# Gathering tokens for 32 experts from two fp32r parts instead of three bf16 parts

## The reference

```
g_idx = argmax(xt @ w_rg + b_rg)                      # 1 group of 4
top_val, top_idx = top_k(e_sel, 2)                    # 2 experts of the group's 8
gates = softmax(g_logits)[g_idx] * softmax(top_val)
# per expert e, over its own tokens xb:
hid = silu(xb @ w_gate[e]) * (xb @ w_up[e])           # 1024 -> 512
y = (hid @ w_down[e]) * gate                          # 512 -> 1024
out = segment_sum(y, token)                           # added back to the tokens' rows
```

## Time and profile before

| | |
|---|---|
| median of 3 runs | 2879.21 us (2877.5 to 2879.88) |
| profiled execution | 2876.93 us, of which 2875.7 us are the span from first to last instruction |
| granted TensorE clock, mean | 0.959 of 2.4 GHz |
| TensorE matmuls busy | 2737.2 us (95%) |
| TensorE weight loads busy | 1894.1 us (66%) |
| VectorE, ScalarE, GpSimd busy | 1221.8, 910.1, 367.7 us |
| moved by DMA | 543.60 MB |

### The profile page before, as it was taken

How to read it: one execution, slowest core, us unless ns; L and a number is a source line. 1 busy time by engine, 2 the same in 40 slices (tenths; PEclk the granted TensorE clock), 3 DMA queues, 4 the chain that set the end, 5 groups by cost and what they waited for, 6 DMA issues and landing times. The chain is left out here.

```text
span 2875.7 us, 36485 instructions
## 1 busy us (share of the span) xinstructions
PE 2737.2 (95%) x14944; PEld 1894.1 (66%) x14944; DVE 1221.8 (42%) x2275; ACT 910.1 (32%) x1666; POOL 367.7 (13%) x197
## 2 busy tenths in 40 slices
PE   7989999999878999999979999999999999999998
PEld 5865455444757545544467767788887776788887
DVE  1542223223755222322246652552553674356254
ACT  4331101111473111111154543442344454343233
POOL 3200000000330000000030011222222001122122
PEclk9989999999988999999999978999999996899999
DMA  5147999998315799999722011223232101123312
GB/s 203 61 188 314 406 402 407 397 406 340 103 44 200 310 406 406 400 402 406 320 85 74 30 59 44 88 88 106 71 109 68 65 17 57 54 79 102 104 59 81
DMA packets 134825, 543.60 MB, mean 189 GB/s; under 512 B 14592, under 2 KB 26112, under 8 KB 85376
## 3 DMA queue, kind: packets, MB, share of 16 engines
q1 hardware_dynamic: 127120, 536.94, 48.4%
q10 hardware_dynamic: 7536, 4.28, 0.5%
HBM read 539.09 MB, written 2.10 MB: 188 GB/s over the span
## 5 line engine op out<-in xcount | busy, mean ns | idle before, releaser
L500 PE MATMUL ps<-w,w 128*128 128x512 f32 x3360 | 769.7, 391 | 19.2 <-POOL w L256 10.1
L500 PEld LDWEIGHTS ps<-w,w 128*128 128x128 f32 x3360 | 632.5, 188 | 153.7 <-DVE w L443 9.8
L256 POOL TENSOR_TENSOR w<-w,w 128x1024 fp32r<-128x1024 f32 (+3 forms) x139 | 339.0, 2450 | 2267.1 <-ACT w L248 2267.1
L502 PE MATMUL ps<-w,w 128*128 128x512 f32 (+2 forms) x2256 | 495.5, 381 | 24.5 <-DVE w L981 15.2
L502 PEld LDWEIGHTS ps<-w,w 128*128 128x128 f32 x2256 | 415.4, 190 | 102.5 <-ACT w L572 15.6
L1185 PE MATMUL ps<-w,w 128*64 128x512 f32 x2048 | 451.6, 594 | 1.8 <-issue 1.8
L248 ACT ACTIVATE w<-w 128x1024 fp32r<-128x1024 f32 (+3 forms) x260 | 251.4, 1000 | 428.0 <-PE ps L500 221.5
L256 DVE TENSOR_TENSOR w<-w,w 128x1024 fp32r<-128x1024 f32 (+3 forms) x121 | 195.2, 1619 | 403.3 <-ACT w L248 400.8
L1185 PEld LDWEIGHTS ps<-w,w 128*64 128x64 f32 x2048 | 146.0, 137 | 285.5 <-issue 285.5
L1410 DVE TENSOR_TENSOR X<-ps,X 128x512 f32<-128x512 f32 x256 | 163.9, 682 | 221.5 <-PE ps L1221 220.5
L1207 PE MATMUL ps<-w,w 128*64 128x512 f32 x1024 | 226.8, 595 | 0.8 <-ACT w L1262 0.8
(11 more groups left out here) (234 smaller groups left out, 2305.4 us busy)
## 6 DMA issues: line engine op xcount, KB each, us to landing
w<-in_moe_w_gate SPq DMA_DIRECT2D x128, 1024.0 KB, 10.2
w<-in_moe_w_up SPq DMA_DIRECT2D x128, 1024.0 KB, 12.9
w<-in_moe_w_down SPq DMA_DIRECT2D x128, 1024.0 KB, 8.1
w<-in_w_up SPq DMA_DIRECT2D x40, 1024.0 KB, 5.1
w<-in_w_down SPq DMA_DIRECT2D x20, 1024.0 KB, 5.1
w<-in_w_in SPq DMA_DIRECT2D x16, 1024.0 KB, 5.1
w<-in_ab_w_in SPq DMA_DIRECT2D x10, 1024.0 KB, 5.1
w<-in_c_w_in SPq DMA_DIRECT2D x8, 1024.0 KB, 5.9
```

The lines of the kernel that those rows point to most:

```text
L256: up(self.wlo[self.low[s][0]], lane.e.tensor_tensor(lo, raw, hi.bitcast(F32), ALU.subtract))
L500: ins = pe.matmul(bank[:, :], wp[:, k, P * o:P * o + P], ap(k0 + k), start=first, stop=stop)
L502: ins = pe.matmul(bank[:, 0:width], ap(k0 + k)[:, P * o:P * o + P], wp[:, k, :], start=first, stop=stop)
```

## The change

The parts of the rows are two fp32r ones: ScalarE makes `HB[0]` (fp32r), VectorE the rest `HB[1]` (fp32r). The one-hot matrix stays bf16 as VectorE writes it; ScalarE copies each pair's `SEL` to an fp32r matrix `SELR` (`scalar_pick`), of which there is one buffer, and the gather reads that. `YH` and `YL` have one buffer instead of two. In the routing, `M8` and `MASK` are computed before the weights of the two choices. The small tiles move in SBUF into the region of the transposed features, and GpSimd's copy of the bf16 identity waits for the masks. The loop for overfull experts is changed in the same way.

```diff
-        HB = [at(2048 * j, 4, 1024, dt=BF16) for j in range(3)]
+        HB = [at(0, 4, 1024, dt=F32R), at(4096, 4, 1024, dt=F32R)]
...
+        SELR = at(S0 + 960, 4, P, dt=F32R)
...
-        YH = [at(10240, 1024, dt=F32R), at(11264, 1024, dt=F32R)]
-        YL = [at(12288, 1024, dt=F32R), at(13312, 1024, dt=F32R)]
+        YH = at(10240, 1024, dt=F32R)
+        YL = at(11264, 1024, dt=F32R)
...
         def tensor_gather(p, j):
-            PE.wait_ge(pick, p + 1)
+            PE.wait_ge(pick_r, p + 1)
...
-                for q in range(3):
+                for q in range(2):
                     for c in range(NT):
                         kk = 4 * j + k
-                        i = pe.matmul(bank[:, P * k:P * k + P], HB[q][:, c, P * kk:P * kk + P], SEL[p % 2][:, c, :],
-                                      start=(q == 0 and c == 0), stop=(q == 2 and c == NT - 1))
+                        i = pe.matmul(bank[:, P * k:P * k + P], HB[q][:, c, P * kk:P * kk + P], SELR[:, c, :],
+                                      start=(q == 0 and c == 0), stop=(q == 1 and c == NT - 1))
...
         def tensor_slots(p):
+            PE.wait_ge(cb_ready, 3)
             PE.wait_ge(gate3, 1)
+            PE.wait_ge(pick, p + 1)
...
+        def scalar_pick(p):
+            S.wait_ge(pick, p + 1)
+            if p:
+                S.wait_ge(bga.full, p)
+                S.wait_ge(bgv.full, p)
+            up(pick_r, act.activation(SELR[:, :, :], SEL[p % 2][:, :, :], ACT.Copy))
...
-            for j in range(2):
-                for c in range(NT):
-                    if j:
-                        S.wait_ge(hb_rest, c + 1)
-                    else:
-                        normed(S, c + 1)
-                    up(hb, act.activation(HB[j][:, c, :], HF[:, c, :], ACT.Copy))
+            for c in range(NT):
+                up(hb, act.activation(HB[0][:, c, :], HF[:, c, :], ACT.Copy))
...
+            scalar_pick(0)
             scalar_gather(0)
             for p in range(PAIRS):
+                if p + 1 < PAIRS:
+                    scalar_pick(p + 1)
                 bank = bg.next(S)
...
-            V.wait_ge(ba.free, 4)
-            for j in range(2):
-                for c in range(NT):
-                    V.wait_ge(hb, 4 * j + c + 1)
-                    dst = HF if j == 0 else HB[2]
-                    ins = dve.tensor_tensor(dst[:, c, :], HF[:, c, :], HB[j][:, c, :], ALU.subtract)
-                    up(h_row if j else hb_rest, ins)
+            for c in range(NT):
+                V.wait_ge(hb, c + 1)
+                up(h_row, dve.tensor_tensor(HB[1][:, c, :], HF[:, c, :], f32(HB[0][:, c, :]), ALU.subtract))
...
             up(rx_in, dve.tensor_tensor(ed, m2, m1, ALU.subtract))
+            vstep(dve.tensor_tensor(M8, O1, O2, ALU.add))
+            up(masks, dve.tensor_tensor(by_group(MASK), M8.unsqueeze(2).to_broadcast([P, 4, 4, 8]), groups, ALU.mult))
             V.wait_next(rx_out)
...
-            for a, name in ((tri_b, "tri"), (ones_b, "ones"), (identb, "ident")):
+            for a, name in ((tri_b, "tri"), (ones_b, "ones")):
                 up(cb_ready, pool.tensor_copy(a, cst(name)))
+            G.wait_ge(masks, 1)
+            up(cb_ready, pool.tensor_copy(identb, cst("ident")))
```

More of the change, by code:

```diff
@@ L1025, in program @@
         handoff(n) for n in ("gate", "up", "gather_act", "gather_dve", "hidden", "down", "slots"))
-    h_normed, cb_ready, hb, hb_rest, h_row = (
-        sig(n) for n in ("h_normed", "cb_ready", "h_bf16", "h_rest", "h_row"))
+    h_normed, cb_ready, hb, h_row = (sig(n) for n in ("h_normed", "cb_ready", "h_hi", "h_lo"))
     rx_in, rx_out, masks, n_ready = (
         sig(n) for n in ("router_exp_in", "router_exp_out", "masks", "n_ready"))
-    pick, st, yhi_w, gate3 = (sig(n) for n in ("pick", "slots_t", "y_hi_w", "gate3"))
+    pick, pick_r, st, yhi_w, gate3 = (sig(n) for n in ("pick", "pick_fp32r", "slots_t", "y_hi_w", "gate3"))
     def plan_moe(layer):
@@ L1075, in moe @@
         late = range(next_half + 3, next_half + SPLITS)
-        HB = [at(2048 * j, 4, 1024, dt=BF16) for j in range(3)]
+        HB = [at(0, 4, 1024, dt=F32R), at(4096, 4, 1024, dt=F32R)]
         HF = HF_[layer]
-        HTF = at((12288, 8192)[layer], KD, T)
+        S0 = (12288, 8192)[layer]
+        HTF = at(S0, KD, T)
         gB, WR = loaded.pop(("moe", layer))
-        CB = at(7168, 3, P, dt=BF16)
-        tri_b, ones_b, identb = CB[:, 0, :], CB[:, 1, :], CB[:, 2, :]
+        identb = at(S0 + 1728, P, dt=BF16)[:, :]
+        CB = at(16384, 2, P, dt=BF16)
+        tri_b, ones_b = CB[:, 0, :], CB[:, 1, :]
         R0 = 17408
@@ L1092, in moe @@
         MASK = at(R0 + 464, 4, 32, dt=BF16)[:, :, :]
[L1093 to L1102, removed]
+        CNT = at(16512, 32)[:, :]
+        CMP = at(16544, 32, NOVER)[:, :, :]
+        gr = at(16768, 2, 4, 32)
+        SID = at(S0, 4, 32)[:, :, :]
+        GATE = at(S0 + 128, 4, 32)[:, :, :]
+        OE = at(S0 + 256, 32)[:, :]
+        OS = at(S0 + 288, 32)[:, :]
+        ON = at(S0 + 320, 32)[:, :]
+        OH = at(S0 + 352, 32)[:, :]
+        scs = at(S0 + 384, 16, 4)
         sc = [scs[:, i, :] for i in range(16)]
@@ L1107, in moe @@
         NI = XR[:, 2 * layer + 1, 0:1].bitcast(I32)
[L1108 to L1111, removed]
-        YH = [at(10240, 1024, dt=F32R), at(11264, 1024, dt=F32R)]
-        YL = [at(12288, 1024, dt=F32R), at(13312, 1024, dt=F32R)]
+        SEL = [at(S0 + 448, 4, P, dt=BF16), at(S0 + 704, 4, P, dt=BF16)]
+        SELR = at(S0 + 960, 4, P, dt=F32R)
+        GATE3 = at(S0 + 1472, 4, 32, 4, dt=BF16)[:, :, :, 0:3]
+        XG = [at((8192, 12288)[layer] + 1024 * j, KD, P) for j in range(2)]
+        YH = at(10240, 1024, dt=F32R)
+        YL = at(11264, 1024, dt=F32R)
         HS = [at(14336, 512), at(14848, 512)]
@@ L1142, in tensor_route @@
             PE.wait_ge(masks, 1)
-            PE.wait_ge(cb_ready, 3)
+            PE.wait_ge(cb_ready, 2)
             bank = banks.take(bv)
@@ L1219, in tensor_combine @@
                 bank = banks.take(bx)
-                pe.matmul(bank[:, :], s_, YH[p % 2][:, 512 * n:512 * n + 512], start=True, stop=False)
-                up(bx.full, pe.matmul(bank[:, :], s_, YL[p % 2][:, 512 * n:512 * n + 512], start=False, stop=True))
+                pe.matmul(bank[:, :], s_, YH[:, 512 * n:512 * n + 512], start=True, stop=False)
+                up(bx.full, pe.matmul(bank[:, :], s_, YL[:, 512 * n:512 * n + 512], start=False, stop=True))
         def tensor():
@@ L1298, in scalar @@
                 for n in range(2):
-                    up(yhi_w, act.activation(YH[p % 2][:, 512 * n:512 * n + 512], bdown.banks[bdown.free.base + 2 * p + n][:, :],
+                    up(yhi_w, act.activation(YH[:, 512 * n:512 * n + 512], bdown.banks[bdown.free.base + 2 * p + n][:, :],
                                              ACT.Identity, scale=GC_[p % 2]))
@@ L1346, in vector_route @@
             vstep(dve.tensor_tensor(p2, p2, gp, ALU.mult))
-            vstep(dve.tensor_tensor(M8, O1, O2, ALU.add))
             vstep(dve.tensor_tensor(O1, O1, bc(p1, [P, 4, 8], 2), ALU.mult))
@@ L1350, in vector_route @@
             vstep(dve.tensor_tensor(E8, O1, O2, ALU.add))
-            up(masks, dve.tensor_tensor(by_group(MASK), M8.unsqueeze(2).to_broadcast([P, 4, 4, 8]), groups, ALU.mult))
             vstep(dve.tensor_tensor(by_group(GATE), E8.unsqueeze(2).to_broadcast([P, 4, 4, 8]), groups, ALU.mult))
@@ L1416, in vector_rest @@
                 V.wait_ge(yhi_w, 2 * p + n + 1)
-                up(bdown.free, dve.scalar_tensor_tensor(YL[p % 2][:, 512 * n:512 * n + 512], bank[:, :], GC_[p % 2],
-                                                        f32(YH[p % 2][:, 512 * n:512 * n + 512]), ALU.mult, ALU.subtract))
+                up(bdown.free, dve.scalar_tensor_tensor(YL[:, 512 * n:512 * n + 512], bank[:, :], GC_[p % 2],
+                                                        f32(YH[:, 512 * n:512 * n + 512]), ALU.mult, ALU.subtract))
         def vector():
@@ L1464, in moe @@
         nblocks = nc.values_load(NI[0:1, 0:1], min_val=0, max_val=2 * T // CAP)
-        SELO = at(16384, 4, P, dt=BF16)
+        SELO = at(16384, 4, P, dt=F32R)
         SGO = at(16896, 4, P)
         STO = at(17408, 512)
-        XGO = at(8192, 8, 64)
-        WO = at(10240, 4096)
-        YO = at(14336, 1024)
+        WO = at((8192, 12288)[layer], 4096)
+        YO = at((14336, 10240)[layer], 1024)
+        XGO = at((15360, 11264)[layer], 8, 64)
         HG = at(18432, 512)
@@ L1516, in moe @@
                     vs_(dve.tensor_scalar(SELO[:, c, 0:CAP], cst("iota"), sc[10][:, c:c + 1], None, ALU.is_equal))
-                    vs_(dve.tensor_scalar(SGO[:, c, 0:CAP], SELO[:, c, 0:CAP], sc[11][:, c:c + 1], None, ALU.mult))
+                    vs_(dve.tensor_scalar(SGO[:, c, 0:CAP], f32(SELO[:, c, 0:CAP]), sc[11][:, c:c + 1], None, ALU.mult))
                 pe.wait_ge(s_loop, n[0])
@@ L1522, in moe @@
```

(2 more changed lines are left out.)

## The result

The changed kernel takes 2943.97 us in the median of 4 runs (2942.91 to 2944.85), the kernel before 2878.94: a ratio of 1.0226, with a 95% interval from 1.0208 to 1.0244. It is 65 us slower; the forecast was 2948 us in a range of 2924 to 3015. The profiled execution took 2943.13 us, 66.2 more than the one of before.

A forecast was written before the change was run, and what follows sets the result against it. TensorE's instruction stream was taken as the bound, not the transfers. Loops +53.7 and first gathers +15.3, the rest 0, gave +69 on the profiled 2876.9: 2946; the median 2.3 above: 2948 us, range 2924 to 3015.

The forecast's parts named there:

- The bound: In the experts' loops, TensorE's instruction stream sets the pair's 31.30 us; the transfers follow at 30.5 us.
- The gather's step: In the loops, 64 fp32r matmuls a pair follow one another every 0.112 us: +1.79 us a pair, +53.7 us.
- The estimate from the Trainium skill: Columns/1.2 ns per load, 107 ns for 128: a pair pays 6.83 us in gathers, the loops +43 us.
- The first gathers: Ahead of each layer's loop, the clock stays low: 13.4 us each, +5.7 and +6.6, 1.5 each behind; together +15.3 us.
- the other case, in which the clock rises: In each layer's first gather, the clock rises at 4.5 us: 9.3 us, +1.6 each, +3 us in all.
- Masks -0.8 us: In the routing, masks computed first remove two VectorE waits of 0.27 and 0.51 us: -0.8 us.
- copy +0.7 us: Ahead of TensorE's first gather, ScalarE's copy to SELR takes 0.60 us and adds a second handover: +0.7 us.
- The copy's cover: In the loop, the copy to SELR lies in ScalarE's 5.54 us idle time: 0; without that cover +18 us.
- the single buffer: One YH and YL in the pairs: the order on TensorE already covers the buffer, 0.
- Fewer copies and subtractions: In the routing, four copies and four subtractions fewer; the router's product is still waited for: 0, at best -0.1.
- rival A: In the gathers, fp32r loads as quickly as bf16; transfers then bind at 30.5 us: -24 us, 2854 us; chance 7%.
- Rival D: In the loops, the clock falls in the gathers: about 2 us a pair, +60 beyond the sum, 3008 us; chance 10%.

## Why the prediction was right

**The bound.** TensorE's stream was read as the length of a pair, from the idle times and not from the DMA share of 1.00. Three lengths of the gather gave three pair steps, 29.52, 31.30 and 32.99 us, each TensorE's own sum, with no idle time between its matmuls in the loop.

**The gather's step.** Taken as 0.112 us between 0.107 and 0.118 (the working gives 0.117); measured 0.110. The loops came to +50.7 us instead of +53.7, this term being 1.69 us a pair instead of 1.79. That the step is not the stream's was argued from the rows with 4, 64 and 260 columns and is shown by the gather with 64. The row with 260 columns was no evidence for it: at 0.227 us for 512 columns, 260 of them stream in 0.115 us, about that row's own 0.120. Its nearness to the other two was a coincidence. That the step is the load's stays argued.

The estimate from the Trainium skill ("TensorE: Matmul & The Clock Gate", section "LDWEIGHTS"), 0.107 us and +43 us, was lower than what was measured. The prediction had left open how a rule of the same page of the Trainium skill, in its section "Weight-path perf modes", treats fp32r. The trace shows it: fp32r loads take 192 ns in the median, as the plain float32 ones of L1740 do, and bf16 loads 99 in the mean.

**The first gathers.** +15.3 us were taken, +16.9 measured: the clock did stay low, 13.92 and 13.91 us against 13.4, and the tail at half speed cost 1.8 and 1.9 us instead of 1.5. The kernel with dense matmuls ahead shows that this is the clock. (For the other case, in which the clock rises, the recorded "+1.6 each, +3 us in all" is wrong for the second layer, where 9.3 against 6.86 us is +2.4; the sum doesn't use it.)

**The small edits.** Masks -0.8 us and copy +0.7 us: both are in the traces. VectorE's one-hot matrix of the first pair, before and after:

```profile
219.25 1.29 DVE L1381 TENSOR_TENSOR w<-CT,w 128x512 bf16<-128x512 f32 x2
```

```profile
218.41 1.29 DVE L1385 TENSOR_TENSOR w<-CT,w 128x512 bf16<-128x512 f32 x2
```

It starts 0.84 us sooner, and the gather follows its start after 1.41 us instead of 0.75; together the gather started 0.18 us sooner (219.82). That the masks' 0.8 us are worth as much in the kernel's time is not shown, since alone they gained nothing. The copy's cover and the single buffer are shown by experiments. Fewer copies and subtractions: VectorE idled 5.1 us for the router's product instead of 0.47, and nothing moved.

**What was off.** The price of rival A. I read 413 GB/s as what the transfers can do, when it was what TensorE asked for; they gave 421 without a wait of TensorE's. A quick fp32r load would have been worth -54 us in the loops and not -24. Rival D did not happen in this kernel, but it did with half the columns. Against it I had the order of the gathers and one stretch of eight matmuls; with no more than that, its staying away is in part luck.

**Not predicted.** -1.2 us between the layers, made of a router's product of layer two that ran more at the full clock (9.88 instead of 12.44 us), transposes ahead of it that did so too (-0.6), and +2.1 us ahead of those. In that last stretch the mean granted clock was 0.92 instead of 0.94, and the same 384 matmuls of L500 took 90.7 instead of 87.9 us: the clock again, in code that was not changed.

**Luck.** Between +69 and the measured 66.2 us lie 3.0 too many in the loops, 1.6 too few in the first gathers, and 1.4 fewer that had no term. The last two nearly cancel by chance.

## What to carry to other kernels

A matmul with a stationary block of its own has a step below which fewer moving columns don't bring it: in fp32r 0.110 us with 128 columns and 0.109 with 64. In bf16 128 columns took 0.056, which is also what they take at the rate of the stream of 512 (0.057). So two thirds of the matmuls took 1.3 times as long. Before counting matmuls, ask which operand is loaded how often; streaming the wide operand past the narrow one, even with transposes behind it, was 2.6 us a pair cheaper. A DMA share of 1.00 doesn't make the transfers the bound or their rate the ceiling: see who waits.

## What was not expected of the hardware

- A stream of matmuls without a pause can lose the full clock: 64 matmuls a pair with 64 columns each let it fall (mean granted clock in the two loops 0.90 and 0.92), where those with 128 columns held 1.00.
- One core's loads ran at 421 to 423 GB/s with a DMA share of 1.01, where the same loads at 413 GB/s had shown 1.00.
- Unchanged code took up to 6 us more in one kernel than in another, from 1456.4 to 1462.2 us behind the last SILU, the longest with the lowest mean granted clock (0.94, the others 0.95). Against that, 0.8 us won on VectorE ahead of a gather at the low clock could not be told: the gather took 8.38 instead of 7.71 us.
